# State read-out of the SSM: sums formed on GpSimd, two products on TensorE per scan in place of four

## The reference, cut to what matters

```python
bu = jnp.einsum("bsgh,gph->bsgp", uf.astype(jnp.complex64), b_bar)
...
_, states = lax.associative_scan(combine, (a_seq, bu), axis=1)
c_mat = lax.complex(c_re.astype(jnp.float32), c_im.astype(jnp.float32))
y = jnp.real(jnp.einsum("bsgp,ghp->bsgh", states, c_mat))
```

## Time and profile before

| | |
|---|---|
| median of 3 runs | 1318.02 us (1315.23 to 1323.71) |
| the profiled execution: its own time / its span | 1315.59 us / 1313.8 us |
| TensorE busy in matmuls | 1189.1 us (91%) |
| VectorE busy | 644.6 us (49%) |
| ScalarE busy | 331.9 us (25%) |
| GpSimd busy | 110.7 us (8%) |
| chain that ended last | TensorE 81%, VectorE 12%, ScalarE 3%, issue 2%, DMA 1% |
| line 1055 on that chain | 2.1% |
| mean granted TensorE clock | 0.933 |

### The profile page before, as it was taken

The page is one execution under the profiler, slowest core; times in us unless marked ns, Lnnn a source line. Parts: engine busy times, 40 slices in busy tenths (PEclk is TensorE's granted clock), DMA queues, the critical chain, the costliest instruction groups (busy, mean ns, idle before and its releaser), DMA issues.

```text
span 1313.8 us, 15287 instructions
## 1 busy us (share of the span) xinstructions
PE 1189.1 (91%) x6130; PEld 828.0 (63%) x6130; DVE 644.6 (49%) x1339; ACT 331.9 (25%) x748; POOL 110.7 (8%) x106
## 2 busy tenths in 40 slices
PE   5999999787878299799997999999799979999998
PEld 2546765775778287355646888844546548888643
DVE  2222014679777855469713555570287514555400
ACT  2212214753543120410402222210301312222100
POOL 0000100210110100026000000010053000000000
PEclk8899999888778587899998999999899989999999
DMA  9631321000001210352235444342422334354320
GB/s 360 214 123 54 128 77 56 1 1 1 2 7 36 87 61 32 128 191 98 64 110 170 146 150 170 128 160 96 154 103 68 125 128 128 128 164 157 131 94 32
DMA packets 97689, 140.05 MB, mean 107 GB/s; under 512 B 12207, under 2 KB 63058, under 8 KB 97490
## 3 DMA queue, kind: packets, MB, share of 16 engines
q1 hardware_dynamic: 96708, 136.84, 30.8%
q10 hardware_dynamic: 910, 2.22, 0.4%
HBM read 138.01 MB, written 1.05 MB: 106 GB/s over the span
## 4 chain that ended last, share of the span: by engine, by line
PE 81%; DVE 12%; ACT 3%; issue 2%; DMA 1%; POOL 0%; SPq 0%; DVEq 0%; ACTq 0%; POOLq 0%
PE bank L1168 23%; PE bank L1185 12%; PE bank L786 11%; PE bank L1010 7%; PE bank L465 3%; PE bank L458 3%; PE bank L1000 2%; PE bank L1055 2%; DVE ring L1905 2%; DMA ring<-in_ada_w 1%; PE bank L1032 1%; PE bank L620 1%; PE bank L597 1%; PE bank L868 1%; PE bank L770 1%
## 5 line engine op out<-in xcount | busy, mean ns | idle before, releaser
L1168 PE MATMUL bank<-work,ring 128*128 128x256 f32 x1152 | 249.8, 379 | 2.6 <-DVE work L2235 2.6
L1168 PEld LDWEIGHTS bank<-work,ring 128*128 128x128 f32 x1152 | 218.7, 190 | 32.9 <-issue 3.3
L2438 DVE SCALAR_TENSOR_TENSOR work<-work,prm 128x256 f32<-128x256 f32 x176 | 77.5, 482 | 150.2 <-ACT work L1600 148.7
L786 PE MATMUL bank<-work,ring 128*128 128x256 f32 (+2 forms) x448 | 144.9, 485 | 2.3 <-ACT work L1238 2.3
L786 PEld LDWEIGHTS bank<-work,ring 128*128 128x128 f32 (+1 forms) x448 | 84.4, 189 | 61.5 <-issue 55.0
L1185 PE MATMUL bank<-ring,work 128*128 128x512 f32 x224 | 96.8, 592 | 0.0
L1598 ACT ACTIVATE work<-bank 128x512 f32<-128x512 f32 x44 | 26.3, 597 | 231.4 <-PE bank L1168 231.4
L1185 PEld LDWEIGHTS bank<-ring,work 128*128 128x128 f32 x224 | 42.6, 190 | 53.6 <-issue 53.6
L2472 POOL TENSOR_TENSOR small<-small,con 128x8 f32<-128x8 f32 (+5 forms) x22 | 33.1, 1507 | 480.4 <-DVE small L2222 126.0
L1010 PE MATMUL bank<-ring,work 128*128 128x512 f32 (+1 forms) x192 | 72.9, 528 | 0.0
L2461 DVE TENSOR_TENSOR xc<-xc,bank 128x512 f32<-128x512 f32 x8 | 5.5, 687 | 112.8 <-PE bank L1185 112.8
(11 more groups left out here) (426 smaller groups left out, 1777.3 us busy)
## 6 DMA issues: line engine op xcount, KB each, us to landing
ring<-in_w_up SPq DMA_DIRECT2D x36, 1024.0 KB, 7.7
ring<-in_w_in SPq DMA_DIRECT2D x24, 1024.0 KB, 7.4
ring<-in_ada_w SPq DMA_DIRECT2D x12, 1024.0 KB, 11.5
ring<-in_w_down SPq DMA_DIRECT2D x12, 1024.0 KB, 6.3
ring<-in_w_out SPq DMA_DIRECT2D x8, 1024.0 KB, 7.3
work<-in_w_up SPq DMA_DIRECT2D x8, 1024.0 KB, 7.8
work<-in_w_down SPq DMA_DIRECT2D x8, 1024.0 KB, 5.9
work<-in_w_in SPq DMA_DIRECT2D x4, 1024.0 KB, 8.5
```

Of the source, the lines that this page charges most:

```text
L786: ins = mm(b[0:rows, 0:toks], wt[:, k, off:off + rows], hT[:, k, 0:toks], start=(k == 0), stop=(k == KD - 1))
L1168: ins = mm(b[:, SEQ * half:SEQ * half + SEQ], wt[:, KD * half + k, P * j:P * j + P], xnT[:, k, :], start=(k == 0), stop=(k == KD - 1))
L2438: ins = STT(out=cv[:, p, half, :], in0=hp[:, p, half, tap:tap + SEQ], scalar=k2(l, "conv01", 1, 44 * tap + FB * half + m), in1=cv[:, p, ha ...
```

## The change

GpSimd now makes, after its two products of a scan (each with one buffer, `pr1` and `pr2`, at a new place), the difference of the halves of `pr1` and the sum of the halves of `pr2`, each 128 x 256. These are the real and the imaginary part of the state; they go to `states`, which holds four scans. Before the difference it waits for its own products (`sum_in`), and before the products of a scan for its own sum of the scan before. It waits for a read-out from s = 4 on, for that of scan s - 4. TensorE reads out in the passes s = 3, 5, 7 and 9 only, two scans at a time, with two products for each scan, in the order: C_re for the first scan, C_re for the second, -C_im for the first, -C_im for the second. The two scans of a pair write different rows of the PSUM bank. ScalarE no longer makes `cT[:, 1]`. `rotated` now counts one for a scan and not two.

```diff
--- before.py
+++ after.py
@@ -171,7 +171,7 @@
 SEMAPHORES = """a_bar_sc act_T cc_zero first_consts hT_even hT_odd ssq_ctx angle angle_raw b_spread bk_ch block_T bonus_in c0 c_masked c_silu c_tanh consts crow d_bias d_hat
  d_rstd d_var d_w decays derived dt_exp e_made ends g_tanh gelu_in gelu_tanh h0 hp_pads k_tok kk_rn kk_sq kkf
  lam_exp lam_sum lora lw_in k_rate m_bias mix_gmlp mix_rw mix_ssm mod_cols off_made off_step out_done p2_load pads
- params_1 params_2 q_tok qk_rot qk_rstd qk_sum qk_var rk_used rotated rotated_used rstd_1 rstd_a rstd_f rstd_lat scanned
+ params_1 params_2 q_tok qk_rot qk_rstd qk_sum qk_var rk_used rotated rotated_used sum_in rstd_1 rstd_a rstd_f rstd_lat scanned
  ssq ssq_a ssq_f t64_diag t_inv tables u_theta us var_1 var_a var_f vec_step vg_n vg_rstd vg_var weights_used
  x1 x_again x_in xs xs_a y_cubic y_gelu y_half y_hat y_rstd y_tanh y_var z_f""".split()
 
@@ -376,7 +376,8 @@
         G0 = M0 + 16640
         m1, m2, xr = take_work(G0, 512), take_work(G0 + 512, 512), take_work(G0 + 1024, 512)
         gs = take_work(G0 + 1536, 2, 512)
-        pr1, pr2 = take_work(G0 + 2560, 2, 512), take_work(G0 + 3584, 2, 512)
+        states = take_work(G0 + 2560, 4, 2, SEQ)
+        pr1, pr2 = take_work(M0 + 5632, 2, SEQ), take_work(M0 + 6144, 2, SEQ)
         qT2, kT2 = take_work(G0 + 1024, 4, SEQ), take_work(G0 + 2048, 4, SEQ)
         H0 = G0 + 4608
         probs = (take_work(M0 + 10496, 4, 2, P), take_work(M0 + 11520, 4, 2, SEQ))
@@ -1047,15 +1048,16 @@
                         if s == 7:
                             wt_g = weights(("in2", l, 3), KD, 512)
                         by_token(3, wt_g, SEQ, SEQ, s - 7, (0, 1))
-                    if s >= 2:
-                        q = s - 2
-                        lo, blk = 32 * (q % 4), q // 4
-                        pe.wait_ge(S["rotated"], 2 * (ST * l + q + 1))
-                        for f, (ct, pr, half) in enumerate(((0, pr1, 0), (1, pr1, 1), (2, pr2, 0), (2, pr2, 1))):
-                            ins = mm(y[lo:lo + 32, SEQ * blk:SEQ * blk + SEQ], cT[:, ct, blk, lo:lo + 32], pr[:, q % 2, SEQ * half:SEQ * half + SEQ],
-                                     start=(f == 0), stop=(f == 3))
-                        if q < ST - 1:
-                            ins.then_inc(S["rotated_used"], 1)
+                    if s >= 3 and s % 2:
+                        pair = (s - 3, s - 2)
+                        for ct, part in ((0, 0), (2, 1)):
+                            for q in pair:
+                                lo, blk = 32 * (q % 4), q // 4
+                                pe.wait_ge(S["rotated"], ST * l + q + 1)
+                                ins = mm(y[lo:lo + 32, SEQ * blk:SEQ * blk + SEQ], cT[:, ct, blk, lo:lo + 32], states[:, q % 4, part, :],
+                                         start=(part == 0), stop=(part == 1), skip_group_check=True)
+                                if part and q < ST - 1:
+                                    ins.then_inc(S["rotated_used"], 1)
                 ins.then_inc(*filling(("ssm_y", l)))
 
                 for c in range(2):
@@ -1471,7 +1473,6 @@
                         act.wait_ge(S["z_f"], 4)
                     b = bank_of(key)
                     A.activation(cT[:, 0].rearrange("p a b -> p (a b)"), b[:, 0:256], ACT.Copy)
-                    A.activation(cT[:, 1].rearrange("p a b -> p (a b)"), b[:, 0:256], ACT.Copy, scale=-1.0)
                     A.activation(cT[:, 2].rearrange("p a b -> p (a b)"), b[:, 256:512], ACT.Copy, scale=-1.0).then_inc(*emptying(key))
                     key = ("bT", l)
                     act.wait_ge(*when_full(key))
@@ -2304,7 +2305,7 @@
                     TT(xr[:, SEQ:512], m2[:, SEQ:512], m2[:, 0:SEQ], SUB).then_inc(S["vec_step"], 1)
                     vec.wait_ge(S["vec_step"], next(vec_steps))
                     if s >= 2:
-                        vec.wait_ge(S["rotated"], 2 * (ST * l + s - 1))
+                        vec.wait_ge(S["rotated"], ST * l + s - 1)
                     for c in range(2):
                         ins = V.tensor_tensor_scan(gs[:, s % 2, SEQ * c:SEQ * c + SEQ], small[:, 440 + s:441 + s].to_broadcast([P, SEQ]),
                                                    xr[:, SEQ * c:SEQ * c + SEQ], 0.0, MUL, ADD)
@@ -2525,11 +2526,16 @@
                         pool.wait_ge(S["qk_var"], 4 * l + i + 1)
                         rsqrt(small[:, 296 + 8 * i:304 + 8 * i], small[:, 264 + 8 * i:272 + 8 * i]).then_inc(S["qk_rstd"], 1)
                     pool.wait_ge(S["scanned"], ST * l + s + 1)
-                    if s >= 2:
-                        pool.wait_ge(S["rotated_used"], (ST - 1) * l + s - 1)
+                    if s >= 4:
+                        pool.wait_ge(S["rotated_used"], (ST - 1) * l + s - 3)
                     g = gs[:, s % 2, :]
-                    G.tensor_tensor(pr1[:, s % 2, :], g, csc[:, s, 0:2, :].rearrange("p a b -> p (a b)"), MUL).then_inc(S["rotated"], 1)
-                    G.tensor_tensor(pr2[:, s % 2, :], g, csc[:, s, 1:3, :].rearrange("p a b -> p (a b)"), MUL).then_inc(S["rotated"], 1)
+                    if s or l:
+                        pool.wait_ge(S["rotated"], ST * l + s)
+                    G.tensor_tensor(pr1.rearrange("p a b -> p (a b)"), g, csc[:, s, 0:2, :].rearrange("p a b -> p (a b)"), MUL).then_inc(S["sum_in"], 1)
+                    G.tensor_tensor(pr2.rearrange("p a b -> p (a b)"), g, csc[:, s, 1:3, :].rearrange("p a b -> p (a b)"), MUL).then_inc(S["sum_in"], 1)
+                    pool.wait_ge(S["sum_in"], 2 * (ST * l + s) + 2)
+                    G.tensor_tensor(states[:, s % 4, 0, :], pr1[:, 0, :], pr1[:, 1, :], SUB)
+                    G.tensor_tensor(states[:, s % 4, 1, :], pr2[:, 0, :], pr2[:, 1, :], ADD).then_inc(S["rotated"], 1)
                 pool.wait_ge(S["vg_var"], l + 1)
                 rsqrt(small[:, 262:264], small[:, 260:262]).then_inc(S["vg_rstd"], 1)
                 for t in range(2):
```

## The result

The changed kernel takes 1341.95 us (median of 4 runs, 1338.44 to 1345.51) against 1318.97 us (1315.23 to 1323.71) for the kernel before: ratio 1.0174, interval 1.0137 to 1.0211. The profiled execution is the slowest of the four (1345.51 us).

The account below looks back on a forecast made before the run. TensorE's chain bounded the loop, with VectorE only 1.2 us a round behind and becoming the bound. Per layer 6.7 up to y plus 2.0 clock, 8.7; twice 17.4, less 0.3: +17.1, median 1335 us, range 1320 to 1345.

Parts of the forecast that it names:

- The lock: VectorE instructions with two SBUF inputs and GpSimd instructions reading SBUF exclude each other; 0.95 us lost per wait for a product.
- the first rival: Even scans and scan 1: lines 2302 and 2304 are not held up by the sums; 1328 us, chance 0.18.
- The sums' length: GpSimd's added difference and sum of 256 elements per scan: 0.70 us each, of it 0.55 with the lock.
- The rotation: VectorE's rotary embedding between scans, alternating with four GpSimd instructions: 5.67 us, against 4.93 with two products beside it.
- The round: VectorE's time for two scans with the rotary embedding: 14.88 us, above TensorE's 13.06 now.
- Up to y: Layer's end: line 2318, which reads the complete y, starts at 634.65 against 627.92, +6.7 us.
- The clock: TensorE's granted clock drops after waiting some 10 us for the last pair: 2.0 us lost a layer.
- ScalarE's copy: One copy per layer removed, 0.38 us long: 0.3 us saved in layer 1, nothing in layer 0.
- The second: Round of two scans: TensorE's time comes back, sums stay out of VectorE's way; -2.7 us a layer, 1312, chance 0.09.
- The third: TensorE paces the loop to the end: -7.4 to -10 us a layer, 1301, chance 0.04.
- The fourth: GpSimd becomes the bound, its sums costing 1.25 us each: 8.8 us a layer, 1352, chance 0.05.
- The fifth: TensorE's read-out: nothing is read together or ahead; overlap worth 0.7 us at layer's end, inside the forecast, no chance given.

Follow-up runs that it names:

- 1: The changed kernel with GpSimd's difference and sum cut from 256 columns to 8: 1324.40 us, ratio 1.0033.
- 2: The changed kernel with the difference and sum replaced by two GpSimd fills that read nothing from SBUF: 1325.99 us, ratio 1.0067.
- 6: The changed kernel with VectorE's rotary embedding moved from behind scans 2, 4, 6 to just before the real scan of scans 3, 5, 7: 1333.54 us, ratio 1.0099.
- experiment 9: The changed kernel with 10 idle TensorE products of 512 columns ahead of each layer's last pair: 1331.49 us, ratio 1.0104.
- experiment 3: The changed kernel without sums: four buffers stay, TensorE reads pairs of scans with four products each: 1324.94 us, ratio 1.0036.
- kernel 7: The kernel before, with TensorE reading two scans at a time; no sums, two buffers: 1319.43 us, ratio 0.9981.
- kernel 10: The changed kernel without sums, four products per scan, rotary embedding moved, scans 6 and 7 read out alone: 1316.25 us, ratio 0.9958.
- kernel 8: The changed kernel without sums, four products per scan in pairs, four buffers, rotary embedding moved: 1321.02 us, ratio 0.9986.

## Why the prediction was right

The forecast was 1335 in a range of 1320 to 1345, slower by 17.1 us; measured are 1341.95 and 23.0. By its own steps:

- **The lock.** The lock that the sum needs is right, and shown by 1, 2 and 6: a GpSimd product or sum and a VectorE instruction with two SBUF inputs wait for one another when both are ready at one time. What the rows before could not show, that lines 2302 and 2304 are caught as well, is so; the first rival, 1328, took them to be free. With products, sums and fills the traces agree with the Trainium skill's rule (SBUF — State Buffer, "Who interferes with whom"), also in that a GpSimd instruction that only writes does not keep such an instruction out (experiment 2).
- **What I read wrongly there.** GpSimd was not idle beside line 2302 of the earlier trace rows, and the trace did not agree wherever it shows such a pair. GpSimd's power -0.5 (line 2472, both inputs in SBUF) runs across lines 2302 (585.07, 0.42 in the earlier trace rows) and 2304, and neither waits:

```profile
584.88 1.64 POOL L2472 TENSOR_TENSOR small<-small,con 128x8 f32<-128x8 f32 x1
```

```profile
585.52 0.42 DVE L2304 TENSOR_TENSOR work<-work 128x256 f32<-128x256 f32 x1
```

In the changed kernel it is the same: line 2281 starts at 594.46 while the power of 592.91 (1.83 us) is still running, and takes 0.67. So not every GpSimd instruction that reads SBUF keeps VectorE out for its whole length. Why the power does not isn't tested; it works on 8 columns. The size in the sum is not touched, as line 2302 takes 0.42 at 575.53 too, where GpSimd does nothing.
- **The sums' length.** Taken at 0.70; the difference takes 0.72 and 0.73 undisturbed, and the sum, which always meets VectorE, 0.90 or more. The Trainium skill's figure (GPSIMD Engine Reference, "Performance versus the Vector engine") gave an estimate of 0.55 us plus dispatch, and 0.72 agrees with that. The wait on `sum_in`, 0.06 by the forecast, shows as a gap of 0.08 to 0.09 us.
- **The rotation** of 5.67 us was met to the hundredth. **The round** was 15.06 and not 14.88: the two waits in the even scan were 0.51 and 0.41, taken as 0.30 and 0.37, which is 0.25 more, and the square totals with line 2275 took 1.37, taken as 1.46. In scan 1 it was not lines 2303 and 2305 that waited but 2305 and the real scan (1.68 us for two in place of 1.27, line 2310), which I had left out: 0.82 for the 0.67 forecast.
- **Up to y** +8.3 and +8.2 us, forecast +6.7. 0.7 is those waits: the last scan ends 54.9 us behind the first product and not 54.3. 0.9 is the clock, which I had put wholly behind y: the last six instructions run at half clock too.
- **The clock** was taken at 2.0 a layer and is 2.4 to 2.9 (experiment 9). With the waits this makes 9.8 and 10.3 in place of 8.7.
- **A pair of eight** was taken at 1.2 us; the first of the layer takes 0.99 (1057 at 597.13, the next instruction at 598.12). It is hidden, as forecast.
- **One sign was not met.** I had written that the medians of lines 2302 and 2304 would be over 0.42. Line 2303 has 0.43, since only the even scans wait, as my own sum had it; the round of 15.06, the waits of TensorE of 4.04 and 9.37 us and the clock of 0.5 behind the second were.
- **ScalarE's copy.** From line 1483 to 1492 it took 939.63 - 930.59 = 9.04 us before and takes 8.79 now, 0.25 for the 0.3 forecast. Nothing is left of it in the profiled execution, since the projection behind it (line 1001) took 9.98 us at a mean clock of 0.71, and 7.14 at 1.00 before.
- **The rivals.** The second had the sums stay out of VectorE's way and TensorE's time come back, 1312. Experiment 1 is its best case, since almost none of the sums' reading is left in it, and it is at 1324.4, not below the kernel before. What the rival overlooked is that the products do more harm once no read-out holds them back (experiment 3). The third fell with 3, where TensorE's work shrinks by half of the read-out and the time does not. The fourth had sums of 1.25 us, and they take 0.72. The fifth is out: TensorE's pairs stand in the timeline.
- **Outside the two loops** are 2.9 us of the 23.0. In the profiled execution the stretch from the up-projection of layer 0 to scan 0 of layer 1 is 254.1 us, before 251.5, and the same stretch is 251.2 to 255.3 in the other kernels, which don't change it. The 2.6 us between the two are the projection at its end, 2.84 longer, less the copy. In the thirteen kernels' traces this projection takes 7.14 us (the kernel before; 2 and 9 within 0.01 of it) to 10.13 us (6), at mean clocks of 1.00 down to 0.70, whether the kernel has the sums or not (3, without them, 8.83). So it looks like a property of the single execution and not of the change, but one trace of each does not show that, and why the medians hold about as much more than the loops stays open.

## What to carry to other kernels

An engine's idle time in a round is only worth what the next engine leaves over, so before shortening TensorE read how full VectorE is in the same stretch (here 11.85 of 13.06 us). Work moved to GpSimd is not free where VectorE reads two operands from SBUF beside it: price it as VectorE's time, or order VectorE so that its PSUM products meet it. And a wait that looks like a cost can be keeping two engines apart; taking it away with more buffers, and the pairs with it, cost 1.4 us up to scan 7 here, and 1.8 against the kernel with the pairs alone.

## What the runs showed of the hardware that was not expected

- The real scan (line 2310) waits for GpSimd too: 1.68 us in place of 1.27 for two of 256 elements beside the sum, and 2.22 beside a product in kernel 7.
- Products to different rows of a PSUM bank, in turn, take 1.85 us for 16 instructions of 256 columns, against 3.68 one scan behind the other.
- The clock did not follow the length of the last pause alone. Behind 1.86 us (kernel 10) it was 1.00. Behind 3.12 (kernel 8) it was 0.50, and already 0.78 in the pause. Behind 4.04 in the changed kernel it was 1.00 for the six instructions that came first (622 to 624) and 0.58 in the two microseconds after them, with TensorE busy throughout; in kernel 9, which is the same up to there, the same six instructions behind the same 4.04 us took 1.91 and not 1.05. Behind 9.37 it was 0.50. Products whose result nobody used, put in the pause, kept it full (experiment 9, 1.00 from 625 on).
- Two SBUF inputs are not the only condition for the wait: line 2274 has one, of 8 columns, and takes 0.76 us beside a product and 0.17 without.
- GpSimd's power of 8 columns kept no instruction of VectorE waiting in the loops of these traces. It takes 1.63 or 1.64 us where it starts clear of VectorE's instructions with two SBUF inputs, and 1.75 to 1.87 where it starts beside one.
